# Hybrid encoder layer on Trainium2: the last input chunks and the branch and mixing weights loaded as 1 MB units with both halves of the split in one slot, and two expert chunks moved ahead of them in the load queue

## The chip, the cores and the metric

The kernel runs on one core of one Trainium2 chip. The metric is the device time of one execution in microseconds (us). The engines named below are TensorE (PE in the profile; PEld is its weight load), VectorE (DVE), ScalarE (ACT), GpSimd (POOL) and SyncE (SP), whose queue issues nearly all loads. All weights are read from HBM in every execution.

## The reference, cut to what is computed

```python
def token_mixer(h, ...):
    proj = h @ w_in + b_in
    q, k, v, xr, yr, gate_logits = jnp.split(proj, SPLITS, axis=-1)
    ...                                   # q/k norm, rotary positions
    attn = block_attention(q, k, v)
    xc = depthwise_conv(xr, conv_w, conv_b)
    lru = rglru(xc, ..., False) + rglru(xc, ..., True)
    rec = lru * jax.nn.gelu(yr, approximate=True)
    g_attn, g_rec = jnp.split(jax.nn.sigmoid(gate_logits), N_BRANCHES, axis=-1)
    merged = g_attn * (attn @ w_attn_o) + g_rec * (rec @ w_lru_o)
    return merged @ w_out
...
    x = x + token_mixer(rmsnorm(x, norm1_g[l]), ...)
    x = x + moe_ffn(rmsnorm(x, norm2_g[l]), ...)   # top 4 of 32 experts, SwiGLU
return rmsnorm(x, final_g)
```

x is 256 tokens by 1024 channels in float32. An expert has 1024x2048 weights going up and 1024x1024 going down, 12.6 MB; 32 experts are 402.7 MB of the 438 MB that are read.

## The kernel before, in words

**Buffers.** The ring is eight slots of 128x4096 float32 (2 MB each), numbered 0 to 7 and allocated in pairs (0,1), (2,3), (4,5), (6,7). LOWS is slot 6 and `wide` is slot 7. `late`, `pbuf`, `xr_flat` and `x_sb` hold other data first and expert weights later.

**First stage.** The mixer's weights come as 15 chunks of 128x4096 from `pre` (chunk 3 is half as wide). Chunks 0, 1 and 4 to 9 are the input projection, four blocks of output channels each: TensorE's `group(i)` for i = 0 to 31 computes block i%4 of its chunk, and `group_done` counts them. Chunks 2 and 3 are q, k and v. Chunks 10, 11 and 13 are the two branches' output matrices, 12 and 14 are `w_out`. Every chunk is split for precision into a high part, rounded to fp32r, and a low part, which is the rest: ScalarE makes the high part in two halves (`split_high`; VectorE does it for chunks 5 and 9), VectorE the low part (`split_low`), and `product` makes three matmuls out of each pair. The chunk lands in an even slot, its low part overwrites it there, and its high part goes into the odd slot beside it (for chunk 13: slot 6 and `late`).

**Around the change.** Chunks 4 to 9 are read by groups 8 to 31. Between the groups stand the attention's scores, transposes and values and the gates of the recurrence. Then TensorE runs `branches(g)` for g = 0 to 7, one block of 128 channels each; VectorE's loop over g multiplies both branch results with the gates, adds them and splits the sum (`merged_ok` counts these). `branches(g)` waits for `merged_ok` g-1, since it writes the PSUM bank of g-2. `mix(c)` multiplies block c of the merged sum into four PSUM banks, and `mix_end(n)` adds the last blocks to bank n. After that come the residual, the router, and the experts.

**Experts.** Expert weights are cut into chunks k of 2 MB, six an expert: four for gate and up, two for down. Chunk k goes to slot `SLOT_ORDER[k % 8]`; chunks 42, 43 and half of 41 have a place of their own in `late`, in `pbuf` and `xr_flat`, and in `x_sb`, and come early. From chunk 8 on `expert_load` waits until TensorE has read the chunk eight before it (`chunk_used`). Later, in the loop, two slots are loaded by one DMA of 4 MB.

**Order.** Each engine's order is written out by hand. SP issues its DMAs in that order and waits before each for what frees its place, so everything behind a waiting DMA waits too. VectorE and ScalarE likewise work strictly in order.

## Time and profile before

| what | value |
|---|---|
| median of 3 runs | 1138.17 us (1135.7 to 1138.58) |
| profiled execution, first to last instruction | 1134.2 us |
| TensorE busy | 1084.8 us (96%) |
| VectorE busy | 371.1 us (33%) |
| ScalarE busy | 237.2 us (21%) |
| read from HBM | 438.20 MB, 387 GB/s over the span |
| mean granted TensorE clock | 0.986 of full |

The metric is the time of a whole execution, the span runs from the first to the last instruction of one profiled execution; the median lies 4.0 us above that span. A share of busy time is an average over stages with different limits, so the stages have to be read one by one: the mixer's (up to about 211 us), the router's (211 to 226 us) and the experts' (from 226 us on). In the chain that ended last, each piece is what the next one waited for.

### The profile page before, as it was taken

Reading aid. Unit: us, or ns where it says so; the run is one execution under the profiler, and the core shown is the slowest. Engines: PE = TensorE matmul, PEld = TensorE weight load, DVE = VectorE, ACT = ScalarE, POOL = GpSimd, SP = SyncE. Lnnn points to the kernel's source line nnn. Section 1 sums busy time; section 2 is a strip of 40 time slices with the busy share of each in tenths; the row PEclk is TensorE's granted clock in tenths of the full one; section 3 lists DMA queues with packets and bytes.
Section 4 is the critical chain, followed back from the end, with each engine's and each line's share of the span. In section 5 each row is a group of like instructions: output and inputs, shape, how many; then the busy total and the mean of one; then the engine's idle time right before and its main releaser. Section 6 shows DMA issues by size and latency. Waiting matters only on the chain.

```text
span 1134.2 us, 12887 instructions
## 1 busy us (share of the span) xinstructions
PE 1084.8 (96%) x5407; PEld 503.4 (44%) x5407; DVE 371.1 (33%) x645; ACT 237.2 (21%) x369; POOL 2.6 (0%) x10
## 2 busy tenths in 40 slices
PE   7999999999999999999998989898989899899987
PEld 7999899633333333333333333333333333333332
DVE  6997887522212222122121211111211212121212
ACT  5399961211111111111111110011110101010102
POOL 0000000000000000000000000000000000000000
PEclk9999999899999999999999999999999999999999
DMA  9544277999999999999999999999999999999996
GB/s 353 185 178 149 84 287 300 419 425 399 431 425 428 426 434 432 433 426 435 431 429 436 430 430 436 429 430 436 430 432 433 429 436 430 427 427 429 426 428 247
DMA packets 25637, 439.77 MB, mean 388 GB/s; under 512 B 3425, under 2 KB 4065, under 8 KB 6273
## 3 DMA queue, kind: packets, MB, share of 16 engines
q1 hardware_dynamic: 24976, 438.27, 91.5%
q10 hardware_dynamic: 624, 0.99, 0.2%
q8 instruction: 27, 0.44, 0.2%
q14 instruction: 10, 0.07, 0.0%
HBM read 438.20 MB, written 1.05 MB: 387 GB/s over the span
## 4 chain that ended last, share of the span: by engine, by line
PE 67%; DMA 28%; DVE 2%; SPq 1%; ACT 1%; issue 0%; DVEq 0%
PE ps L1491 26%; DMA slots<-in_w_down_dram 22%; PE ps L1500 13%; PE ps L1172 13%; DMA slots<-in_w_gu_dram 5%; PE ps L1455 5%; PE ps L1436 3%; PE ps L1549 2%; DVE slots_r L725 1%; SPq L403 1%; PE ps L1229 1%; PE ps L1450 1%; PE ps L1414 1%; PE ps L1234 0%; PE ps L1526 0%; PE ps L1274 0%
## 5 line engine op out<-in xcount | busy, mean ns | idle before, releaser
L1500 PE MATMUL ps<-slots,lru 128*64 128x512 f32 x1024 | 239.8, 610 | 17.2 <-DMA slots<-in_w_down_dram 17.2
L1491 PE MATMUL ps<-slots,lru 128*64 128x512 f32 x1024 | 227.7, 594 | 11.7 <-DMA slots<-in_w_gu_dram 11.2
L1491 PE MATMUL ps<-slots,qT 128*64 128x512 f32 x984 | 223.8, 596 | 4.6 <-DMA slots<-in_w_gu_dram 4.6
L1491 PEld LDWEIGHTS ps<-slots,lru 128*64 128x64 f32 x1024 | 74.1, 137 | 160.8 <-issue 139.7
L1491 PEld LDWEIGHTS ps<-slots,qT 128*64 128x64 f32 x984 | 68.9, 137 | 152.2 <-issue 144.8
L1500 PEld LDWEIGHTS ps<-slots,lru 128*64 128x64 f32 x1024 | 68.5, 139 | 142.5 <-issue 123.5
L1100 DVE COPY lru<-ps 128x512 f32<-128x512 f32 x32 | 22.1, 692 | 322.9 <-PE ps L1491 322.9
L1172 PE MATMUL ps<-slots_r 128*128 128x256 f32 (+1 forms) x812 | 107.7, 291 | 0.2 <-DVE slots_r L725 0.2
L1172 PEld LDWEIGHTS ps<-slots_r 128*128 128x128 f32 x812 | 102.2, 191 | 5.4 <-issue 2.5
L653 ACT ACTIVATE lru<-ps 128x512 f32<-128x512 f32 x32 | 19.1, 598 | 395.3 <-PE ps L1491 395.3
L1082 DVE TENSOR_SCALAR lru<-sq,rank_col,small 128x64 f32<-128x64 f32 x64 | 17.2, 312 | 241.8 <-PE ps L1436 241.8
L1455 PE MATMUL ps<-lru 128*128 128x512 f32 x136 | 65.5, 605 | 0.9 <-DVE lru L1135 0.9
L1108 DVE TENSOR_TENSOR lru<-ps,cst 128x1024 f32<-128x1024 f32 x32 | 39.2, 1225 | 74.3 <-PE ps L1549 74.3
L1436 PE MATMUL ps<-hn,lru 128*64 128x512 f32 x256 | 62.7, 608 | 0.9 <-DVE lru L1020 0.9
L725 DVE TENSOR_TENSOR slots_r<-slots,slots_r 128x4096 fp32r<-128x4096 f32 (+1 forms) x16 | 62.0, 3888 | 3.6 <-ACT slots_r L440 3.4
L645 ACT ACTIVATE lru<-ps 64x512 f32<-64x512 f32 x63 | 37.3, 592 | 123.0 <-PE ps L1500 122.3
L655 ACT ACTIVATE lru<-lru 128x512 f32<-128x512 f32 x32 | 20.2, 631 | 149.6 <-DVE lru L1112 149.6
L440 ACT ACTIVATE slots_r<-slots 128x2048 fp32r<-128x2048 f32 (+1 forms) x24 | 43.4, 1840 | 36.5 <-DMA slots<-in_pre_dram 36.5
L638 ACT ACTIVATE qT<-ps 128x512 f32<-128x512 f32 x32 | 19.1, 598 | 137.5 <-PE ps L1436 137.5
L1549 PEld LDWEIGHTS ps<-sq,lru 128*128 128x128 f32 x256 | 34.8, 197 | 29.3 <-DVE lru L1100 18.5
L1549 PE MATMUL ps<-sq,lru 128*128 128x128 f32 x256 | 41.9, 314 | 0.0
L1455 PEld LDWEIGHTS ps<-lru 128*128 128x128 f32 x136 | 23.2, 190 | 31.5 <-issue 29.7
(200 smaller groups left out, 649.3 us busy)
## 6 DMA issues: line engine op xcount, KB each, us to landing
slots<-in_w_gu_dram SPq DMA_DIRECT2D x40, 4096.0 KB, 29.2
slots<-in_w_gu_dram SPq DMA_DIRECT2D x44, 2048.0 KB, 18.9
slots<-in_w_down_dram SPq DMA_DIRECT2D x20, 4096.0 KB, 28.4
slots<-in_w_down_dram SPq DMA_DIRECT2D x22, 2048.0 KB, 20.8
slots<-in_pre_dram SPq DMA_DIRECT2D x13, 2048.0 KB, 8.2
slots<-in_w_down_dram SPq DMA_DIRECT2D x8, 512.0 KB, 31.0
slots<-in_pre_dram SPq DMA_DIRECT2D x3, 1024.0 KB, 6.9
slots<-in_w_gu_dram SPq DMA_DIRECT2D x3, 1024.0 KB, 17.4
```

The costliest lines, as they stand in the source:

```text
L440: nc.scalar.activation(high(c)[:, i * w:(i + 1) * w], whole(c)[:, i * w:(i + 1) * w], ACT.Copy).then_inc(split_hi, 1)
L645: nc.scalar.activation(pair_out[i // 2 % 2][rs, side * BANK:(side + 1) * BANK], ps[64 * side:64 * side + 64, bank, :], ACT.Copy).then_inc( ...
L655: nc.scalar.activation(as3(sig), gv[:, :, 0, :], ACT.Sigmoid, scale=ALPHA).then_inc(sig_ok, 1)
L725: return nc.vector.tensor_tensor(dst, whole, hi.bitcast(f32), ALU.subtract)
L1100: nc.vector.tensor_copy(gu_sb[:, 0:BANK], ps[:, 4, :]).then_inc(gu_v, 1)
L1108: nc.vector.tensor_tensor(gub.rearrange("p (j n) -> p j n", j=16), ps[:, 4:6, :].rearrange("p b (j n) -> p (b j) n", n=CAP), bias.unsqueez ...
L1172: ins = nc.tensor.matmul(dst, st[a], mv[b], start=start and q == 0 and k == 0, stop=stop and q == 2 and k == len(sides) - 1)
L1436: ins = nc.tensor.matmul(ps[64 * h:64 * h + 64, 7, :], sel_next[:, t, :], x2[:, t, h * BANK:(h + 1) * BANK], start=(t == 0), stop=(t == T ...
L1455: return nc.tensor.matmul(ps[:, n, :], sgT[pair][:, n // 2, :], pair_out[pair][:, (n % 2) * BANK:(n % 2 + 1) * BANK], start=False, stop=last)
L1491: ins = nc.tensor.matmul(ps[64 * side:64 * side + 64, 4 + b, :], xgT[i % 2][:, k, :], rows[r][:, o:o + BANK], start=(k == 0), stop=(k == K ...
L1500: ins = nc.tensor.matmul(ps[64 * side:64 * side + 64, bank, :], actT[(i - 1) % 2][:, k, :], w[:, r, side * BANK:(side + 1) * BANK], start= ...
L1549: ins = nc.tensor.transpose(ps[:, 4 + j // 4, j % 4 * P:(j % 4 + 1) * P], gu_sb[:, j::KD], ident)
```

## The change

1. Chunks 0 to 7 stay as they are. Chunks 8 to 14 become 14 units of 1 MB, two a chunk, each in one slot: it lands in the slot's first half, where its low part overwrites it, and its high part goes into the second half. Units 0 to 3 are chunks 8 and 9 (groups 24 to 31), units 4 to 9 the branch weights, units 10 to 13 `w_out`.
2. A half of chunk 8 or 9 is 256 columns out of each 512, so that units 0 to 3 are read from HBM in rows of 1 KB.
3. Units 0 to 7 use slots 4, 5, 0, 1, 4, 5, 0, 1. That leaves the pair (2,3) free when chunk 7 has been read, and expert chunks 0 and 1 are issued there, after `group_done` 24, ahead of units 4 to 13.
4. SP's order, what each load waits for, and `SLOT_ORDER` change with it. The load of `late` and that of `pbuf` now stand ahead of unit 7.
5. VectorE's low parts come one unit at a time after the merge of each g but 3, where before a whole chunk came after g = 1, 3 and 7.
6. TensorE runs `branches(0)` to `branches(7)` in a row and then `mix(0)` to `mix(5)`, where `mix(0)` stood after `branches(3)`; `mix_end` has two blocks a bank instead of four. The number of matmuls is the same.

```diff
-        SLOT_ORDER = [2, 3, LOWS, SLOTS - 1, 0, 1, 4, 5]
-        EARLIER = [5, 0, 4, 0, 5, 0, 1, 1]
-        FREED = {2: [(branch_ps, 3)], 0: [(mixed_ps, 1)], LOWS: [(branch_ps, KD)], 4: [(mixed_ps, 2)]}
+        CHUNKS, UNIT = 8, CH // 2
+        PLACE = [2 * (c % PAIRS) for c in range(CHUNKS)]
+        UNITS = [(8, 0), (8, 1), (9, 0), (9, 1), (10, 0), (10, 1), (11, 0), (11, 1), (13, 0), (13, 1),
+                 (12, 0), (12, 1), (14, 0), (14, 1)]
+        UNIT_SLOT = [4, 5, 0, 1, 4, 5, 0, 1, LOWS, 4, 5, 0, 1, LOWS]
+        UNIT_FREED = [(group_done, 16), (group_done, 16), (group_done, 20), (group_done, 20), (group_done, 26),
+                      (group_done, 28), (group_done, 30), (group_done, 32), (gate_ps, 32), (branch_ps, 2),
+                      (branch_ps, 3), (branch_ps, 4), (branch_ps, 6), (branch_ps, 7)]
+        BR_UNIT, MIX_UNIT = 4, 10
+
+        SLOT_ORDER = [2, 3, 4, 5, 0, 1, LOWS, SLOTS - 1]
+        EARLIER = [PLACE.count(s) + UNIT_SLOT.count(s) for s in range(SLOTS - 1)] + [1]
+        FREED = {2: (group_done, 24), 4: (branch_ps, KD), 5: (mixed_ps, 1), 0: (mixed_ps, 2), 1: (mixed_ps, 3),
+                 LOWS: (mixed_ps, 4)}
...
-            for c in range(1, PRE):
-                if c == 13:
-                    sp.wait_ge(group_done, 32)
-                    sp.wait_ge(gate_ps, 32)
-                elif c == 14:
-                    sp.wait_ge(pv_ps, NQ // 2)
-                    half_load(extra_rows(1, 0), EXTRA[1], 0, extra_full[1])
-                    half_load(wide[:, 0:2048], 3, 0, slot_full[SLOTS - 1])
-                    for k in range(2):
-                        expert_load(k)
-                    sp.wait_ge(branch_ps, 6)
-                elif c >= PAIRS:
+            def unit_load(u):
+                sp.wait_ge(*UNIT_FREED[u])
+                dst = kn(unit_whole(u)) if u < BR_UNIT else unit_whole(u)
+                sp.dma_start(dst, unit_src(u)).then_inc(slot_full[UNIT_SLOT[u]], 16)
+
+            for c in range(1, CHUNKS):
+                if c >= PAIRS:
                     sp.wait_ge(*CONSUMED[c - PAIRS])
...
-            expert_load(2)
-            half_load(wide[:, 2048:], 3, 1, slot_full[SLOTS - 1])
+            for u in range(4):
+                unit_load(u)
+            for k in range(2):
+                expert_load(k)
+            for u in range(4, 7):
+                unit_load(u)
+            sp.wait_ge(rec_ok, 2)
+            sp.wait_ge(pv_ps, NQ // 2)
             n, j = step_of(EXTRA[0])
             sp.dma_start(late[:, :], expert_src(n, j)).then_inc(extra_full[0], 16)
-            for k in (4, 5):
-                expert_load(k)
+            half_load(extra_rows(1, 0), EXTRA[1], 0, extra_full[1])
+            unit_load(7)
+            unit_load(8)
+            half_load(wide[:, 0:2048], 7, 0, slot_full[SLOTS - 1])
+            for u in range(9, 14):
+                unit_load(u)
+            expert_load(2)
+            half_load(wide[:, 2048:], 7, 1, slot_full[SLOTS - 1])
             sp.wait_ge(merged_ok, KD)
             half_load(extra_rows(1, 1), EXTRA[1], 1, extra_full[1])
-            for k in RING_CHUNKS[6:SLOTS]:
+            for k in range(3, SLOTS - 1):
                 expert_load(k)
...
             recurrent_high(0)
-            split_high(10, [0])
+            unit_split_high(4)
             group_pair(26)
             pair_probs(3)
-            split_high(10, [1])
+            unit_split_high(5)
             group_pair(28)
             recurrent_high(1)
-            split_high(11, [0])
             attention_high()
+            unit_split_high(6)
             group_pair(30)
-            split_high(11, [1])
             load_sqrt_table(2)
-            for c in range(12, PRE):
-                split_high(c)
+            for u in range(7, len(UNITS)):
+                unit_split_high(u)
...
-            split_low(10)
+            unit_split_low(4)
+            unit_split_low(5)
             recurrent_low(1)
             attention_low()
-            split_low(11)
+            unit_split_low(6)
...
-                if g == 1:
-                    split_low(12)
-                if g == 3:
-                    split_low(13)
-                if g == KD - 1:
-                    split_low_by_halves(14)
+                if g != 3:
+                    unit_split_low(7 + g if g < 3 else 6 + g)
...
-            BLOCKS = CH // P
-            w_br = [chunk(c, BLOCKS) for c in BR_CHUNK]
+            BLOCKS = UNIT // P
+
+            w_br = [unit(u, BLOCKS) for u in range(BR_UNIT, MIX_UNIT)]
...
-                for i, c in enumerate(BR_CHUNK[:2]):
-                    if g > 0 and first <= BLOCKS * i < first + 12:
-                        chunk_in(c)
...
+                u = BR_UNIT + (first + KD - 1) // BLOCKS
...
+                product(half(4 + g % 2, 1), recurrent, ahead=((unit_high_ok(u),), (unit_low_ok(u),), ()))
+                u = BR_UNIT + (first + 11) // BLOCKS
+                product(half(4 + g % 2, 0), attention, ahead=((unit_high_ok(u),), (unit_low_ok(u),), ())
+                        ).then_inc(branch_ps, 1)
+
+            ENDS = 6
...
-                if c == 3:
+                if c % 2 == 1:
                     ins.then_inc(mixed_ps, 1)
...
             def mix_end(n):
-                for c in range(4, KD):
+                if n == 0:
+                    pe.wait_ge(*unit_low_ok(MIX_UNIT + 3))
+                for c in range(ENDS, KD):
...
-            for g in range(4):
+            for g in range(KD):
                 branches(g)
-            mix(0)
-            for g in range(4, KD):
-                branches(g)
-            for c in range(1, 4):
+            for c in range(ENDS):
                 mix(c)
```

The load queue before, from chunk 10 of the mixer's weights (first row) on. slots0 to slots3 are the four pairs, `in_pre` the mixer's weights, `in_w_gu` an expert's:

```order
L339 DMA slots0<-in_pre_dram 128x4096 [waits group_done]
L339 DMA slots1<-in_pre_dram 128x4096 [waits group_done]
L339 DMA slots2<-in_pre_dram 128x4096 [waits group_done]
L339 DMA slots0<-in_pre_dram 128x4096 [waits group_done]
L339 DMA slots3<-in_pre_dram 128x4096 [waits lru_gate_ps,group_done]
L324 DMA pbuf<-in_w_gu_dram 128x2048 [waits pv_ps]
L324 DMA slots3<-in_w_gu_dram 128x2048
L320 DMA slots1<-in_w_gu_dram 128x4096 [waits branch_ps]
L320 DMA slots1<-in_w_gu_dram 128x4096
L339 DMA slots2<-in_pre_dram 128x4096 [waits branch_ps]
L320 DMA slots3<-in_w_gu_dram 128x4096 [waits branch_ps]
```

And now, from units 0 and 1 (first row):

```order
L361 DMA slots2<-in_pre_dram 128x8x256 [waits group_done] x2
L361 DMA slots0<-in_pre_dram 128x8x256 [waits group_done] x2
L352 DMA slots1<-in_w_gu_dram 128x4096 [waits group_done]
L352 DMA slots1<-in_w_gu_dram 128x4096
L361 DMA slots2<-in_pre_dram 128x2048 [waits group_done] x2
L361 DMA slots0<-in_pre_dram 128x2048 [waits group_done]
L396 DMA late<-in_w_gu_dram 128x4096 [waits pv_ps,recurrent_ok]
L356 DMA pbuf<-in_w_gu_dram 128x2048
L361 DMA slots0<-in_pre_dram 128x2048 [waits group_done]
L361 DMA slots3<-in_pre_dram 128x2048 [waits lru_gate_ps]
L356 DMA slots3<-in_w_gu_dram 128x2048
L361 DMA slots2<-in_pre_dram 128x2048 [waits branch_ps] x2
```

Two expert chunks now stand right behind unit 3, and 3 MB for `late` and `pbuf` stand between unit 6 and unit 7 (the row that waits for group_done again).

VectorE before, from the low part of chunk 11 (the second chunk of branch weights) to that of chunk 12. The five 128x256 rows are one merge:

```order
L725 TENSOR_TENSOR slots2_r<-slots2,slots2_r 128x4096 [waits chunk_high]
L961 SCALAR_TENSOR_TENSOR lru<-hn,ps 128x256 [waits branch_ps]
L963 SCALAR_TENSOR_TENSOR lru<-xr_flat,ps 128x256
L965 TENSOR_TENSOR lru<-lru 128x256 [waits v_step]
L722 CAST lru_r<-lru 128x256 [waits v_step]
L725 TENSOR_TENSOR lru_r<-lru,lru_r 128x256 [waits v_step]
L961 SCALAR_TENSOR_TENSOR lru<-hn,ps 128x256 [waits branch_ps]
L963 SCALAR_TENSOR_TENSOR lru<-xr_flat,ps 128x256
L965 TENSOR_TENSOR lru<-lru 128x256 [waits v_step]
L722 CAST lru_r<-lru 128x256 [waits v_step]
L725 TENSOR_TENSOR lru_r<-lru,lru_r 128x256 [waits v_step]
L725 TENSOR_TENSOR slots0_r<-slots0,slots0_r 128x4096 [waits chunk_high]
```

And now, from the low part of unit 6 to the second merge:

```order
L764 TENSOR_TENSOR slots0_r<-slots0,slots0_r 128x2048 [waits chunk_high]
L1004 SCALAR_TENSOR_TENSOR lru<-hn,ps 128x256 [waits branch_ps]
L1006 SCALAR_TENSOR_TENSOR lru<-xr_flat,ps 128x256
L1008 TENSOR_TENSOR lru<-lru 128x256 [waits v_step]
L761 CAST lru_r<-lru 128x256 [waits v_step]
L764 TENSOR_TENSOR lru_r<-lru,lru_r 128x256 [waits v_step]
L764 TENSOR_TENSOR slots0_r<-slots0,slots0_r 128x2048 [waits chunk_high]
L1004 SCALAR_TENSOR_TENSOR lru<-hn,ps 128x256 [waits branch_ps]
L1006 SCALAR_TENSOR_TENSOR lru<-xr_flat,ps 128x256
L1008 TENSOR_TENSOR lru<-lru 128x256 [waits v_step]
L761 CAST lru_r<-lru 128x256 [waits v_step]
L764 TENSOR_TENSOR lru_r<-lru,lru_r 128x256 [waits v_step]
```

A low part, that of unit 7, now stands between the first merge and the second; before, both merges stood ahead of the next low part.

## Rows read from the trace of the kernel before

**Rows 1.** Page, section 2: what all DMA moved, in 40 slices of 28.4 us
```profile
GB/s 353 185 178 149 84 287 300 419 425 399 431 425 428 426 434 432 433 426 435 431 429 436 430 430 436 429 430 436 430 432 433 429 436 430 427 427 429 426 428 247
```

**Rows 2.** Stages: length, each engine's busy us (count), TensorE clock, DMA share, GB/s
```profile
165.00:211.00 46.00, 46.00 (x303) 42.27 (x302) 30.21 (x45) 10.69 (x9) 0.00 (x0) 1.00 0.86 345
211.00:226.00 15.00, 13.69 (x67) 7.29 (x65) 8.77 (x34) 4.61 (x10) 0.00 (x0) 0.77 1.00 421
226.00:276.00 50.00, 49.79 (x218) 17.41 (x220) 13.79 (x37) 5.31 (x8) 0.00 (x0) 1.00 1.00 410
276.00:531.00 255.00, 255.00 (x1165) 89.51 (x1160) 53.97 (x108) 28.49 (x48) 0.00 (x0) 1.00 1.01 429
531.00:1080.00 549.00, 518.67 (x2311) 185.76 (x2310) 112.39 (x220) 57.79 (x96) 0.00 (x0) 0.98 1.00 431
```

**Rows 3.** Chain that ended last, 500 to 640 us: start, us, what
```profile
527.51 3.61 PE ps L1491 x16
531.27 26.39 DMA slots<-in_w_down_dram
```

**Rows 4.** Timeline of the load queue: issue start, us, what, count
```profile
250.46 5.48 SPq L320 DMA_DIRECT2D slots<-in_w_gu_dram  x2
261.28 5.83 SPq L320 DMA_DIRECT2D slots<-in_w_down_dram  x2
272.18 3.76 SPq L320 DMA_DIRECT2D slots<-in_w_gu_dram  x2
```

**Rows 5.** Loads issued at 250.46, 266.78, 272.18, 275.62: count, KB, us to landing
```profile
slots<-in_w_gu_dram SPq DMA_DIRECT2D x1, 2048.0 KB, 8.7
slots<-in_w_down_dram SPq DMA_DIRECT2D x1, 2048.0 KB, 8.5
slots<-in_w_gu_dram SPq DMA_DIRECT2D x1, 2048.0 KB, 8.0
slots<-in_w_gu_dram SPq DMA_DIRECT2D x1, 2048.0 KB, 9.5
```

**Rows 6.** Same view: issued at 124.09, 63.06, 154.57 and 155.04
```profile
slots<-in_pre_dram SPq DMA_DIRECT2D x1, 2048.0 KB, 7.8
slots<-in_w_lru_dram SPq DMA_DIRECT2D x1, 1024.0 KB, 4.8
pbuf<-in_w_gu_dram SPq DMA_DIRECT2D x1, 1024.0 KB, 15.4
slots<-in_w_gu_dram SPq DMA_DIRECT2D x1, 1024.0 KB, 17.4
```

**Rows 7.** Timeline of VectorE: start, us, line, what, shapes, count, [idle before]
```profile
156.41 4.42 DVE L725 TENSOR_TENSOR slots_r<-slots,slots_r 128x4096 fp32r<-128x4096 f32 x1 [1.58 <-ACT slots_r L440]
160.76 0.41 DVE L961 SCALAR_TENSOR_TENSOR lru<-hn,ps 128x256 f32<-128x256 f32 x1
162.32 0.43 DVE L725 TENSOR_TENSOR lru_r<-lru,lru_r 128x256 fp32r<-128x256 f32 x1
193.73 4.49 DVE L725 TENSOR_TENSOR slots_r<-slots,slots_r 128x2048 fp32r<-128x2048 f32 x2
```

**Rows 8.** Timeline of ScalarE, same columns
```profile
140.15 0.84 ACT L460 ACTIVATE xr_flat<-ps,cst 128x256 f32<-128x256 f32 x2
154.46 1.92 ACT L440 ACTIVATE slots_r<-slots 128x2048 fp32r<-128x2048 f32 x1
```

**Rows 9.** Timeline of TensorE, same columns
```profile
146.67 1.08 PE L1298 MATMUL ps<-pbuf,late 128*64 128x256 f32 x8
147.68 6.01 PE L1172 MATMUL ps<-slots_r 128*128 128x256 f32 x48
153.53 2.08 PE L1172 MATMUL ps<-lru_r,slots_r 128*128 128x256 f32 x16
157.85 2.08 PE L1172 MATMUL ps<-lru_r,slots_r 128*128 128x256 f32 x16
162.89 2.14 PE L1172 MATMUL ps<-lru_r,slots_r 128*128 128x256 f32 x16 [0.56 <-DVE lru_r L725]
```

More of the change, by code:

```diff
@@ L578, in _ @@
             lru_gates(1, [0])
-            split_high(8, [0])
+            unit_split_high(0)
             pair_exps(0)
@@ L1177, in chunk, with unit @@
                 return [b.rearrange("p (k n) -> p k n", k=k) for b in (high(c), low(c))]
+            def unit(u, k):
+                return [b.rearrange("p (k n) -> p k n", k=k) for b in (unit_high(u), unit_low(u))]
             def transposes(rows, tp0):
```

103 lines of the change are left out of this document (59 added, 44 removed).

## The prediction

> **What bounds the kernel now.** I read the GB/s line of the page first. From the eighth slice on (199 us) the DMA moves 399 to 436 GB/s to the end [rows 1]: all weights have to come in, and the end is the moment at which the last of them can have come. The stages say more [rows 2]. From 276 us on the DMA is busy all the time at 429 to 431 GB/s. TensorE is too until 531 us (255.00 of 255.00 us); after that it waits 30 us in 549. The chain that ended last is TensorE until 531.1 us and a load from 531.27 us on [rows 3]. So the experts' stage is bound by the DMA once its queue is full, and the question is when that begins. It doesn't begin at 199 us: between 226 and 276 us the DMA makes 410 GB/s, 19 below the 429 that follow, 0.95 MB or 2.2 us of idle, while TensorE is busy 49.79 of 50 us [rows 2].
>
> The load queue shows why [rows 4, 5]. A load of 2 MB with nothing ahead of it lands after 7.8 us [rows 6]. Those issued at 250.46, 266.78 and 272.18 us land after 8.7, 8.5 and 8.0 us, so next to nothing stands ahead of them, and they are issued when TensorE frees their slots: each waits for a `chunk_used`. The one issued at 275.62 lands after 9.5 us, at 285.1, which is 4.9 us behind the 280.2 of the one before. From there the queue grows. **The pinch is at 266 to 272 us**: there the end is set by the moment at which TensorE gives back a slot, and from there by 4.9 us for each 2 MB. TensorE is at that point at the end of an unbroken row of work: 46.00 of 46 us in the mixer, 13.69 of 15 in the router, 49.79 of 50 in the first experts [rows 2].
>
> **The change part by part.**
>
> *The head start.* Expert chunks 0 and 1 are issued at `group_done` 24, 124.1 us (where chunk 10 is issued now), instead of at `branch_ps` 3, 162.89 + 4.3 = 167.2 us [rows 9]. That is 4 MB, or 2 x 4.9 = 9.8 us of DMA work moved into time in which the DMA idles. 13 MB are then left of what is loaded before chunk 8 (21 MB in all, of which chunks 0 and 1, `late`, `pbuf` and half a chunk in `wide` have landed). The first 2 MB are issued when the branches end, near 189.5 us, and land at 197.3; the other 11 MB at 2.45 us each end near 224.3 us. Chunk 8, though, waits for TensorE to have read chunk 0, some 4 us after 226 us (16 matmuls of a chunk take 3.6 us [rows 3]). The DMA has nothing to do between 224.3 and 230, and at 250 to 272 us it waits for slots as before, only longer. I price the head start at nothing: the load at 272.18 us can't be issued earlier than its slot is read, and it now lands within 8.0 - 7.8 = 0.2 us of what an empty queue gives. Bounds: 0 to -0.2 us. What counts is only how far TensorE's timeline moves.
>
> *Units 0 to 3.* Read in rows of 1 KB instead of 16 KB. No row shows 1 KB rows in bulk. They are issued with the 2 MB loads that they replace, units 2 and 3 at `group_done` 20, and unit 3 is used by group 30, ten groups or at least 29 us later (two groups take 6.0 us [rows 9]). Even a landing three times as long as the usual 7.8 us is in time. Nothing, bounds 0 and 0; the ten groups are the cover.
>
> *Units 4 to 6.* Unit 4 waits for `group_done` 26, near 131 us (124.1, some values of 1.1 and two groups of 6.0), and lies behind the two expert chunks: 124.1 + 7.8 = 131.9, 136.8 for the second, 139.3 for the unit. ScalarE waits for it and casts for 1.92 us [rows 8] to 141.2; its copies of groups 26 and 27 then come 1.1 us later than the 140.15 of now. TensorE needs them for group 30, at 147.7 [rows 9]. Nothing. Unit 5 lands at 140.1 + 4.8 = 144.9 [rows 6], unit 6 at 146.7 + 4.8 = 151.5, both cast before groups 30 and 31 end at 153.6.
>
> *The low parts after the groups.* Now VectorE starts chunk 11's low part at 156.41, after a wait of 1.58 for ScalarE, and ends at 160.8; the merge that follows ends at 162.75, and TensorE starts `branches(2)` at 162.89 [rows 7, 9]. Its step is 157.85 - 153.53 = 4.32 us, so it was ready at 162.17: 0.72 us lost. With units, the low part of unit 6 is done at 157.1 (half the work, ScalarE's cast ends at 153.4) and the first merge at 160.0. **-0.72 us.**
>
> *The low part of unit 7, ahead of the second merge.* This is new. Unit 7 may be issued at `group_done` 32, 153.7 us, when `late` (2 MB) and `pbuf` (1 MB), issued at 147.8 when the last values end [rows 9], stand ahead of it. `late` lands 4.9 us behind unit 6, at 156.4; `pbuf` at 158.9; unit 7 at 161.4 (a queued 1 MB costs 155.04 + 17.4 - 154.57 - 15.4 = 2.5 us [rows 6]). ScalarE's cast ends at 163.3, VectorE's low part of 2.25 us (half of 4.49 [rows 7]) at 165.6. Only then comes the second merge, 162.75 - 160.76 = 1.99 us, to 167.6. `branches(3)` waits for it; TensorE is ready at 162.17 + 4.32 = 166.49 and starts at 167.75 (0.14 us after the merge, as now). **+1.26 us**, which nothing hides. If the unit lands up to 1.26 us earlier the stall is gone; 1 us later, it is 2.3.
>
> *The later units.* Per g VectorE has 1.99 + 2.25 = 4.24 us of work less 0.1 of overlap against TensorE's 4.32: it keeps up but gains nothing back. Unit 8 lands at 163.9, unit 9 (issued at 162.3, half a chunk ahead) at 168.9, 10 to 13 when `branch_ps` 3, 4, 6 and 7 are up, 4.8 us later each: all cast before their turn. `branches(4)` needs the third merge at 171.9 and is ready at 172.1. Bounds 0 to +1 us; I take 0, as the sum leaves 0.2 to 0.3 us a step.
>
> *The order of mix.* The same matmuls in another order. `mix_end` has half the work a bank, so VectorE's residuals of 1.1 us follow each other at 1.3 us instead of 2.6; the last still starts when the last bank ends. Nothing; up to +0.3 us if the transposes wait for the second residual.
>
> *A rule on sizes.* The halves of 1 MB queue at 2.5 us each, 421 GB/s [rows 6]. The Trainium skill (DMA: Bandwidth & Descriptors, section Bandwidth) gives 341 GB/s for 1 MB and speaks for larger transfers, which is against this change. By it `pbuf` and unit 7 would each take 3.1 us, the stall would be 2.5 us instead of 1.26, and the time 1.2 us longer; the trace doesn't bear it out for queued loads.
>
> **The sum.** -0.72 + 1.26 = +0.54 us at the pinch, and the same at the end, since all behind it is DMA at a fixed pace: 1134.2 + 0.5 = 1134.7 us for the profiled span. The median of the runs lies 4.0 us above that span, and the runs themselves spread over 2.9 us: 1138.17 + 0.5 = 1138.7 us.
>
> **The rivals.**
>
> *A, my forecast (0.58).* A stall of about 1.3 us moves from one branch to the next and the head start is lost at the pinch: 1138.7 us.
>
> *B, no new stall (0.20).* Unit 7 comes earlier, or VectorE is quicker. TensorE gains 0.72 and the pinch up to 0.2 more: 1137.3 us. For it: landings of single loads differ by half a microsecond.
>
> *C, the head start lasts (0.08).* If the DMA were the bound from 199 us on, as the GB/s line alone suggests, 9.8 us would come off: 1128.4 us. Against it stand the 410 GB/s before 276 us and the landings of 8.0 to 8.7 us. For it: TensorE would have to reach its first experts earlier too, which only a clock that stays up in the router's stage could give: it is at 0.77 there over 15 us [rows 2], so at 1.2 GHz for some 6.9 us, worth up to 3.4 us.
>
> *D, slower (0.14).* TensorE falls to 1.2 GHz once more. Its clock fell in this trace during the router's stage, behind thin work with gaps of under 1 us. A stall of 1.26 us at 166.5 us, with others added if VectorE's margin of 0.2 us a step doesn't hold, may do the same within the branches, where every matmul is on the path. A fall as long as that one costs half of 6.9 us: 0.5 + 3.4 = +3.9, 1142.1 us. It decides from a stall that is long enough to make the clock fall; the present 0.72 us did not.
>
> **How the numbers follow.** A measurement of this kernel can tell 0.3% (3.4 us) from no change: below 1134.8 is faster, above 1141.6 slower. A and B lie within (0.78), C is faster (0.08), D slower (0.14). The range takes in A and B with the spread of the runs (1135.7 to 1138.6 around the median) and the unit's landing 1 us late or more: 1135.5 to 1141.5 us.
>
> **What would show it.** In the profile after: a wait of TensorE for VectorE's merge near 166.5 us, of about 1.3 us, and none at 162.2; expert chunks 0 and 1 issued near 124 us; a DMA that idles near 225 to 230 us and moves fewer than 410 GB/s between 226 and 276 us; loads there that land after 7.8 to 8 us; and the same 429 to 431 GB/s behind it. I am wrong if the load that is issued at 272.2 us now is issued more than 2 us earlier or later, or if the gap between 276 us and the end changes.

## The result and the profile after

| | before | after |
|---|---|---|
| median | 1138.17 us (1135.7 to 1138.58) | 1141.87 us (1140.9 to 1142.57) |
| ratio | 1 | 1.0039, 95% interval 1.0028 to 1.0049 |
| profiled execution, first to last instruction | 1134.2 us | 1140.4 us |
| TensorE's first matmul on chunk 0 | 13.65 us | 13.78 us |
| TensorE begins the experts | 226.21 us | 229.84 us |
| load at the pinch lands | 280.19 us | 285.68 us |

The change makes the kernel 0.39% slower, 4.4 us by the ratio, where 0.5 us were predicted; it came out in the direction of rival D, and a little beyond the range. Both medians are of five runs; the three of before in the table ahead are among them. The profiled execution of after took 1142.15 us as a whole, 1.75 above its span, so of the 4.0 us between span and median of before some 2.2 us are a profiled execution that lay at the fast end of its runs. The 6.2 us between the two spans are therefore not the effect; the ratio is. Two executions far off all others, one of before beside the less_mix kernels below (2821.02 us) and one of merges_first_long_rows (1226.41 us), are left out of the ratios.

First TensorE in the branches, from the timeline of after (start, us, what, count, idle before it and what ended it):

```profile
162.29 2.08 PE L1211 MATMUL ps<-lru_r,slots_r 128*128 128x256 f32 x16
164.21 1.12 PE L1211 MATMUL ps<-slots_r 128*128 128x256 f32 x8
165.17 1.12 PE L1211 MATMUL ps<-lru_r,slots_r 128*128 128x256 f32 x8
166.13 0.64 PE L1211 MATMUL ps<-qT_r,slots_r 128*128 128x256 f32 x4
169.28 3.02 PE L1211 MATMUL ps<-lru_r,slots_r 128*128 128x256 f32 x16 [2.51 <-DVE lru_r L764]
172.10 1.81 PE L1211 MATMUL ps<-slots_r 128*128 128x256 f32 x8
...
175.18 2.08 PE L1211 MATMUL ps<-lru_r,slots_r 128*128 128x256 f32 x16
```

The wait of [rows 9] at 162.89 is gone: `branches(2)` starts at 162.29, 0.6 us sooner. `branches(3)` could start its recurrent part 0.48 us behind 166.13, at 166.61, and starts at 169.28: 2.67 us lost, where +1.26 stood in the sum. And its matmuls behind the wait take 3.02 us for 16 where 2.08 was usual. The windows show why; the columns are busy us (count) of TensorE, its weight loads, VectorE, ScalarE and GpSimd, then granted clock, DMA share and GB/s:

```profile
170.30:173.60 3.30, 3.30 (x18) 3.30 (x17) 3.20 (x7) 1.91 (x1) 0.00 (x0) 0.50 0.30 122
221.50:228.20 6.70, 5.72 (x14) 1.35 (x15) 3.88 (x17) 0.99 (x3) 0.00 (x0) 0.50 0.99 413
...
230.00:233.40 3.40, 3.40 (x18) 1.11 (x18) 1.73 (x12) 0.00 (x0) 0.00 (x0) 1.00 0.00 0
234.50:280.00 45.50, 45.50 (x200) 15.87 (x198) 11.72 (x23) 5.66 (x9) 0.00 (x0) 1.00 0.99 388
280.00:531.00 251.00, 251.00 (x1148) 88.35 (x1144) 54.05 (x108) 28.12 (x47) 0.00 (x0) 1.00 1.01 430
```

TensorE's clock fell to half (1.2 of 2.4 GHz) 1.0 us behind the end of the 2.5 us wait. It was at half from 170.25 to 173.66, 3.41 us. `branches(4)` starts 175.18 - 169.28 = 5.90 us behind `branches(3)` where 4.32 is usual, so the fall costs 1.6 us. The fall in the router's stage is there as before, 6.83 us long. From 230.0 to 233.4 us no DMA moves anything, and from 280 on it moves the 430 GB/s of before.

What ended VectorE's wait, and ScalarE's ahead of it:

```profile
159.74 0.43 DVE L764 TENSOR_TENSOR lru_r<-lru,lru_r 128x256 fp32r<-128x256 f32 x1
165.02 2.29 DVE L764 TENSOR_TENSOR slots_r<-slots,slots_r 128x2048 fp32r<-128x2048 f32 x1 [4.85 <-ACT slots_r L481]
167.23 0.41 DVE L1004 SCALAR_TENSOR_TENSOR lru<-hn,ps 128x256 f32<-128x256 f32 x1
...
168.80 0.43 DVE L764 TENSOR_TENSOR lru_r<-lru,lru_r 128x256 fp32r<-128x256 f32 x1
```

```profile
163.08 1.91 ACT L481 ACTIVATE slots_r<-slots 128x2048 fp32r<-128x2048 f32 x1 [6.88 <-DMA slots<-in_pre_dram]
165.57 1.91 ACT L481 ACTIVATE slots_r<-slots 128x2048 fp32r<-128x2048 f32 x1 [0.58 <-DMA slots<-in_pre_dram]
```

VectorE has nothing to do from 160.17 to 165.02 but to wait for unit 7's high part, and the second merge (167.23 to 169.23) stands behind its low part. ScalarE waited for the load. The loads of `late`, `pbuf` and unit 7 were issued at 147.97, 148.34 and 153.84 us:

```profile
late<-in_w_gu_dram SPq DMA_DIRECT2D x1, 2048.0 KB, 8.9
...
pbuf<-in_w_gu_dram SPq DMA_DIRECT2D x1, 1024.0 KB, 12.2
...
slots<-in_pre_dram SPq DMA_DIRECT2D x1, 1024.0 KB, 9.2
```

They landed at 156.89, 160.57 and 163.06 us. Unit 7 is 2.49 behind `pbuf`, as the sum has it, but `pbuf` is 3.68 behind `late` instead of 2.5. What the DMA did in these 3.7 us:

```profile
DMA packets 205, 1.56 MB, mean 421 GB/s; under 512 B 16, under 2 KB 16, under 8 KB 16
## 3 DMA queue, kind: packets, MB, share of 16 engines
q1 hardware_dynamic: 204, 1.54, 99.2%
q8 instruction: 1, 0.02, 1.7%
```

It was not slower: 421 GB/s, 1.56 MB for a load of 1 MB. A load counts as landed when the last of the 16 engines is done with its share, and the trace has a time for each: for `pbuf` 15 were done by 159.38 us, within 0.7 us of one another, and the last at 160.57. Unit 7 shows the same, 161.88 and 163.06, and so do the two loads behind it; one engine stays 1.2 us behind while the others go on. One 16 KB packet of instructions (q8) stood in this stretch; the packet records put it at 157.71 us with 1.02 us, where a packet of the weights takes 0.61. The same 3.3 to 4.0 us, with one engine 0.8 to 1.7 us behind and an instruction packet at 156.4 to 157.8, are in the eight kernels below that keep this order of loads. That this packet is the cause is read from the times; no run moves it. It doesn't always show: in before one of 1.02 us at 174.43 us left the interval of two loads at 4.89, since one engine was already 1.0 us behind (at 161.53 and 162.56 the last two were done with the load issued at 153.72). The 2.5 us of [rows 6] are intervals of loads that all carry that same delay.

Last, the loads issued at 254.09, 264.91, 275.81 and 279.25 us, which answer to [rows 5]:

```profile
slots<-in_w_gu_dram SPq DMA_DIRECT2D x1, 2048.0 KB, 10.0
...
slots<-in_w_down_dram SPq DMA_DIRECT2D x1, 2048.0 KB, 10.1
...
slots<-in_w_gu_dram SPq DMA_DIRECT2D x1, 2048.0 KB, 9.9
...
slots<-in_w_gu_dram SPq DMA_DIRECT2D x1, 2048.0 KB, 11.3
```

With the two between them (issued at 259.24 and 270.41) they take 9.9 to 10.3 us up to the pinch, where 8.0 to 8.9 were usual. So the pinch moves by more (5.5 us) than TensorE does (3.6).

### The profile page after: what moved, and what is told of

It reads as the page before. It is cut to its first block, busy times and chain, and to the rows that moved or that the text cites. A ratio compares the mean times of both kernels' runs of the same rounds, so it can differ in the third digit from the quotient of the medians.

```text
span 1140.4 us, 12909 instructions
## 1 busy us (share of the span) xinstructions
PE 1081.7 (95%) x5407; PEld 502.0 (44%) x5407; DVE 372.3 (33%) x652; ACT 237.8 (21%) x369; POOL 2.3 (0%) x10
## 4 chain that ended last, share of the span: by engine, by line
PE 66%; DMA 29%; DVE 2%; SPq 1%; ACT 1%; issue 0%; DVEq 0%
PE ps L1536 26%; DMA slots<-in_w_gu_dram 15%; PE ps L1211 13%; PE ps L1545 13%; DMA slots<-in_w_down_dram 12%; PE ps L1500 5%; PE ps L1481 3%; PE ps L1594 2%; SPq L442 1%; DVE slots_r L764 1%; PE ps L1276 1%; PE ps L1495 1%; DMA slots<-in_pre_dram 1%; PE ps L1460 1%; PE ps L1281 1%; PE ps L1571 0%
## 5 line engine op out<-in xcount | busy, mean ns | idle before, releaser
L1536 PEld LDWEIGHTS ps<-slots,lru 128*64 128x64 f32 x1024 | 71.7, 137 | 165.0 <-issue 134.5
L1545 PEld LDWEIGHTS ps<-slots,lru 128*64 128x64 f32 x1024 | 67.8, 137 | 139.9 <-issue 112.4
L1211 PE MATMUL ps<-slots_r 128*128 128x256 f32 (+1 forms) x832 | 111.1, 293 | 0.2 <-DVE slots_r L764 0.2
L1211 PEld LDWEIGHTS ps<-slots_r 128*128 128x128 f32 x832 | 105.6, 193 | 5.4 <-issue 2.9
L764 DVE TENSOR_TENSOR slots_r<-slots,slots_r 128x2048 fp32r<-128x2048 f32 (+1 forms) x23 | 67.2, 2938 | 7.0 <-ACT slots_r L481 6.6
L1594 PE MATMUL ps<-sq,lru 128*128 128x128 f32 x256 | 38.9, 298 | 0.0
L1481 PEld LDWEIGHTS ps<-hn,lru 128*64 128x64 f32 x256 | 19.4, 139 | 35.4 <-issue 34.4
```

The costliest lines, as they stand in the source:

```text
L764: return nc.vector.tensor_tensor(dst, whole, hi.bitcast(f32), ALU.subtract)
L1211: ins = nc.tensor.matmul(dst, st[a], mv[b], start=start and q == 0 and k == 0, stop=stop and q == 2 and k == len(sides) - 1)
L1481: ins = nc.tensor.matmul(ps[64 * h:64 * h + 64, 7, :], sel_next[:, t, :], x2[:, t, h * BANK:(h + 1) * BANK], start=(t == 0), stop=(t == T ...
L1536: ins = nc.tensor.matmul(ps[64 * side:64 * side + 64, 4 + b, :], xgT[i % 2][:, k, :], rows[r][:, o:o + BANK], start=(k == 0), stop=(k == K ...
L1545: ins = nc.tensor.matmul(ps[64 * side:64 * side + 64, bank, :], actT[(i - 1) % 2][:, k, :], w[:, r, side * BANK:(side + 1) * BANK], start= ...
L1594: ins = nc.tensor.transpose(ps[:, 4 + j // 4, j % 4 * P:(j % 4 + 1) * P], gu_sb[:, j::KD], ident)
```

## The experiments

All kernels do the reference's work whole but the two named "less_mix". Differences are ratios to before, each measured beside runs of before on the same chip. A start of the experts is counted from TensorE's first matmul on chunk 0, since that lay anywhere between 12.65 and 14.39 us in the profiled executions.

### Which wait costs it: VectorE's order

Theory T: the low part of unit 7 ahead of the second merge makes the wait, the wait makes the clock fall, and the rest is as before. Rival R: the added transfers and short rows cost it anyway. Four kernels are after with one edit. `merges_first` keeps both first merges ahead of the low part:

```diff
-                if g != 3:
-                    unit_split_low(7 + g if g < 3 else 6 + g)
+                if g > 0:
+                    unit_split_low(6 + g)
```

> The kernel after, with VectorE's second merge ahead of the low part of unit 7 (low parts 7 to 13 after the merges of g = 1 to 7); no load is touched. T: the second merge ends near 164.4 us, TensorE has no wait in the branches, the clock stays up, experts from 225.5 us on, 1137.5 us. R: no load changes, so nothing changes: 1141.9.

Measured: 1136.68 us (1135.79 to 1137.76), ratio 0.9996 (0.9986 to 1.0006). The wait is gone; the timeline of TensorE:

```profile
165.31 1.12 PE L1211 MATMUL ps<-lru_r,slots_r 128*128 128x256 f32 x8
166.27 0.64 PE L1211 MATMUL ps<-qT_r,slots_r 128*128 128x256 f32 x4
166.75 2.08 PE L1211 MATMUL ps<-lru_r,slots_r 128*128 128x256 f32 x16
168.67 1.12 PE L1211 MATMUL ps<-slots_r 128*128 128x256 f32 x8
```

T holds: one line of VectorE's order is worth 0.43%, 4.9 us, and the transfers and 1 KB rows that R blames are still there. Yet nothing is won over before, although the experts begin 1.4 us sooner; more of that below. Of the 1.4 us, 0.8 lie ahead of the router, near the 0.72 predicted for the low parts; the other 0.6 are the router's stage, where the clock fell for 3.41 us in this execution and for 6.83 in that of before.

`stall_filled` leaves the wait and gives TensorE 22 transposes of the identity into a free bank in it:

```diff
             for g in range(KD):
+                if g == 3:
+                    filler(2, 22)
                 branches(g)
```

> The kernel after, with 22 transposes of the identity into an unused bank between branches(2) and branches(3), some 2.4 us of TensorE work that fills the wait for the second merge. T with the clock as a part of it: the wait is filled and the clock doesn't fall at 170 us; experts from 228.3 us on instead of 229.8, the time 1.5 us shorter, 1140.4. If the fall of the clock cost nothing: 1141.9, or more by what the filler overruns. R: 1141.9.

Measured: 1139.92 us (1138.71 to 1141.55), ratio 1.0028 (1.0018 to 1.0038). Timeline and windows:

```profile
166.59 2.56 PE L1421 MATMUL ps<-sq 128*128 128x128 f32 x22
169.32 2.18 PE L1211 MATMUL ps<-lru_r,slots_r 128*128 128x256 f32 x16 [0.17 <-DVE lru_r L764]
...
173.74 2.08 PE L1211 MATMUL ps<-lru_r,slots_r 128*128 128x256 f32 x16
```

```profile
170.00:174.00 4.00, 4.00 (x36) 4.00 (x35) 3.90 (x7) 2.89 (x2) 0.00 (x0) 1.00 0.30 121
224.60:227.90 3.30, 2.94 (x10) 1.24 (x10) 0.90 (x4) 0.27 (x1) 0.00 (x0) 0.50 0.70 283
```

The branches wait as long as in after, behind work that nobody needs, and the clock stays up: `branches(4)` starts 4.42 us behind `branches(3)`, not 5.90. The wait, then, makes the clock fall. By the ratios 1.3 us come off, with two intervals that just overlap (1.0028 to 1.0049 and 1.0018 to 1.0038). The experts begin 2.0 us sooner: 1.4 of it is there when mix begins, and 0.6 comes in the router's stage, where the fall is 3.41 us long instead of 6.83 in this execution, which the edit doesn't touch. So of the 3.5 us by which the experts of after are late, 1.4 to 1.6 are the clock's fall in the branches; the rest is the wait, less the 0.72 won.

`unit7_first` loads units 7 and 8 ahead of `late` and `pbuf`:

```diff
+            unit_load(7)
+            unit_load(8)
             sp.wait_ge(rec_ok, 2)
...
             half_load(extra_rows(1, 0), EXTRA[1], 0, extra_full[1])
-            unit_load(7)
-            unit_load(8)
```

> The kernel after, with the loads of units 7 and 8 issued ahead of those of late and pbuf. Theory T (the end follows the moment at which TensorE reaches the experts): unit 7 lands near 158.7 us, the 2.5 us wait of TensorE for the second merge is gone, the clock doesn't fall near 170 us, the experts start near 225.5 us instead of 229.8, and the time is 0.6 us under the kernel before: 1137.5. Rival R (the loss lies in the loads: rows of 1 KB, halves of 1 MB, a queue that runs dry): the loads are the same in number and size and two of the large ones come later, so the time stays at 1141 to 1143.

Measured: 1145.28 us (1143.8 to 1146.86), ratio 1.0068 (1.0046 to 1.009), 8 us away from what I expected. Timelines of TensorE and of VectorE:

```profile
180.93 3.79 PE L1211 MATMUL ps<-lru_r,slots_r 128*128 128x256 f32 x16 [5.79 <-DVE lru_r L764]
```

```profile
176.67 2.29 DVE L764 TENSOR_TENSOR slots_r<-slots,slots_r 128x2048 fp32r<-128x2048 f32 x1 [6.53 <-ACT slots_r L481]
```

The first wait is gone. But the 3 MB now stand ahead of unit 9, which lands at 174.70 instead of 170.50 and whose low part stands ahead of the fourth merge: the same wait two units later, twice as long, with the clock at half for 6.83 us from 179.93, 1.0 us before the wait ends. I had looked only at the unit that was late.

`chunks_late` takes the head start back, with the two expert chunks behind unit 9:

```diff
-            for k in range(2):
-                expert_load(k)
             for u in range(4, 7):
...
-            for u in range(9, 14):
+            unit_load(9)
+            for k in range(2):
+                expert_load(k)
+            for u in range(10, 14):
```

> The kernel after, with expert chunks 0 and 1 issued behind unit 9, near 162 us, instead of near 124 us. T: the head start of 4 MB is worth nothing as long as TensorE reaches the experts when it does; unit 4 lands 3 us sooner, unit 7 where it did; the stall stays, 1141.9 us within 1. If the head start were worth its bytes (9.8 us), the time would be 1151. R: a queue that runs dry less in front of the experts would give some of its loss back, 1139 to 1141.

Measured: 1143.23 us (1142.43 to 1143.87), ratio 1.0055 (1.0036 to 1.0073). The wait stays, 2.76 us, so the head start doesn't cause it; a second of 0.85 us comes at 189.02, behind unit 10, which stands behind the two chunks now. The same edit on merges_first:

> merges_first with expert chunks 0 and 1 issued behind unit 9 instead of ahead of unit 4. T alone: experts from 225.1 us on, or 0.9 us later if unit 10 is late for its low part; 1136.7 to 1137.6 us as merges_first. Rival Q (a queue that runs dry costs by itself: merges_first starts its experts 1.1 us sooner than the kernel before and is no faster): here the DMA isn't idle at 226 to 229 us any more, the loads at 250 to 276 us land after 8 to 9 us instead of 9.2 to 10, and 1.4 us come off, 1135.3.

Measured: 1144.01 us (1143.47 to 1144.98), ratio 1.007 (1.005 to 1.0089), far off. Timelines of TensorE, VectorE and ScalarE:

```profile
188.36 3.78 PE L1212 MATMUL ps<-lru_r,slots_r 128*128 128x256 f32 x16 [5.16 <-DVE lru_r L765]
```

```profile
184.11 2.29 DVE L765 TENSOR_TENSOR slots_r<-slots,slots_r 128x2048 fp32r<-128x2048 f32 x1 [7.29 <-ACT slots_r L482]
```

```profile
182.16 1.91 ACT L482 ACTIVATE slots_r<-slots 128x2048 fp32r<-128x2048 f32 x1 [10.36 <-DMA slots<-in_pre_dram]
```

Unit 10 lands at 182.14, TensorE comes to the merge behind it sooner, waits 5.16 us, and the clock falls within the wait, at 185.57, for 6.83. As a test of the head start both kernels are spoiled; as a test of the mechanism they are three more cases of it.

`before_low_early` makes the same wait in the kernel before, by order alone: the low part of chunk 12 after g = 0 instead of g = 1.

```diff
-                if g == 1:
+                if g == 0:
                     split_low(12)
```

> The kernel before, with the low part of chunk 12 ahead of VectorE's second merge instead of behind it; no load is touched. T: the chunk lands at 162.6 us, its cast ends at 166.3, its low part at 170.8, the second merge at 172.8; branches(3) starts 5.5 us late (172.9 instead of 167.3), and the clock falls for 3.4 or 6.8 us, 1.7 or 3.4 us more: the time is 6 to 9 us longer, 1142.5 to 1145.5 where the kernel before has 1136.3. R (loads alone decide): 1136.3.

Measured: 1145.28 us (1143.83 to 1146.06), ratio 1.0075 (1.0055 to 1.0095). TensorE waits from 166.88 to 172.52, and the clock is at half for 6.83 us from 168.75, 3.1 us of it behind the wait:

```profile
162.33 2.15 PE L1172 MATMUL ps<-lru_r,slots_r 128*128 128x256 f32 x16 [0.56 <-DVE lru_r L725]
...
172.52 3.52 PE L1172 MATMUL ps<-lru_r,slots_r 128*128 128x256 f32 x16 [5.64 <-DVE lru_r L725]
```

### Where the head start goes

Theory S: TensorE's freeing of slots sets the pace at the pinch, so that 4 MB more in place are worth nothing as long as TensorE begins no sooner. The test is to make it begin sooner, in both kernels, by leaving one of the three products out of every `mix` (32 matmuls of 128x512, 6.9 us; `product` skips the terms that are not named).

```diff
-                               start=(c == 0), stop=(c == KD - 1))
+                               start=(c == 0), stop=(c == KD - 1), terms=(0, 2))
```

> The kernel before, with the low part of the merged sum left out of the mix: 32 of the 96 matmuls of 128x512 less, 32 x 0.216 = 6.9 us of TensorE work less (the output lacks that term). Experts from 219.3 us on instead of 226.2. Theory T (the end follows the moment at which TensorE reaches the experts, as long as the loads before are done by then): here the DMA is still busy with the loads ahead of the experts until 234.5 us, so the 6.9 us can't all be passed on; what it loses at 250 to 276 us comes back, 2 to 3 us: 1133.5 to 1134.5 us where the kernel before has 1136.3. If the end followed TensorE alone: 1129.4.

> merges_first with the same 32 matmuls left out of the mix (the output lacks that term). Experts from 218.2 us on instead of 225.1. T with the head start: the 4 MB that come early are worth something only now, since the DMA would have finished the loads ahead of the experts by some 226 us: the 6.9 us are passed on nearly whole, 1130 to 1131 us where merges_first has 1136.7. If the head start were worth nothing in any case, this kernel and before_less_mix would gain the same.

Measured: before_less_mix 1132.9 us (1131.86 to 1133.89), ratio 0.9964 (0.995 to 0.9978); merges_first_less_mix 1128.48 us (1128.17 to 1129.54), ratio 0.9933 (0.9914 to 0.9953). Without the head start 4.1 us come back of 4.8 by which the experts begin sooner; with it 7.6 of 7.5 (against merges_first 7.2 of 6.1). The two kernels differ by 3.5 us in time and by 2.7 in the start of the experts, so the times alone don't show a worth of the head start.

The landings do. Counted from TensorE's first matmul on chunk 0, the load at the pinch lands at 266.54 us in before and 264.88 in before_less_mix, 1.7 sooner; it lands at 266.37 in merges_first and 259.79 in merges_first_less_mix, 6.6 sooner. In before_less_mix the loads follow one another without a gap from 234.58 us on: the DMA is the bound there. So the head start has a worth, and it is only seen when TensorE comes early enough to use it. From that landing to the end of the span it is 853.3 to 854.9 us in all fourteen profiled executions, so the landing at the pinch decides the span. (The profiled pair of before and before_less_mix is accordingly 2.1 us apart; the ratio says 4.1 with an interval of 3 us. This isn't settled better.)

The pace of the DMA between 234.5 and 280 us, in one window of before, before_less_mix, merges_first, merges_first_less_mix, and merges_first_reload (below), same columns as above:

```profile
234.50:280.00 45.50, 45.50 (x200) 15.84 (x198) 10.73 (x19) 5.52 (x8) 0.00 (x0) 1.00 1.00 407
```

```profile
234.50:280.00 45.50, 45.50 (x200) 15.82 (x198) 11.72 (x23) 6.11 (x9) 0.00 (x0) 1.00 1.01 428
```

```profile
234.50:280.00 45.50, 45.50 (x200) 15.83 (x198) 11.03 (x21) 5.83 (x9) 0.00 (x0) 1.00 0.99 391
```

```profile
234.50:280.00 45.50, 45.50 (x200) 15.71 (x200) 10.82 (x22) 5.23 (x8) 0.00 (x0) 1.00 0.99 402
```

```profile
234.50:280.00 45.50, 45.50 (x200) 15.84 (x198) 11.66 (x23) 6.13 (x9) 0.00 (x0) 1.00 0.99 391
```

The engines are busy all the time in all of them, and yet move 388 (in after) to 428 GB/s: at the start of a load single packets of 16 KB take over 0.8 us instead of 0.61, 64 of them in before, up to 1.3 us, and 84 in merges_first, up to 2.6. In before_less_mix, where each load is issued over 6 us before the one ahead of it lands (these take 11 to 13 us), there are 3, and every load lands 4.88 to 4.91 us behind the last. In the others, with loads issued 2 to 5 us ahead, it is anything from 4.9 to 7.3. A deep queue is no warrant: in merges_first a load issued at 286.55 us, 8.4 ahead, landed 6.23 behind the last, with one engine 1.3 us behind the others and an instruction packet at 298.61. Between before and merges_first the windows differ by 16 of 407 GB/s over 45.5 us, 1.8 us, and it eats the 1.4 us that TensorE gains: the load at the pinch lands only 0.17 us sooner.

Theory Q: this comes from the queue's having stood empty from 226 to 230 us. `merges_first_reload` keeps it full there by reading 2 MB twice:

```diff
             half_load(x_flat, HALF, 1, half_full)
+            sp.wait_ge(extra_full[1], 32)
+            half_load(extra_rows(1, 1), EXTRA[1], 1, extra_full[1])
+            half_load(extra_rows(1, 0), EXTRA[1], 0, extra_full[1])
```

> The kernel merges_first (1136.7) with two more loads of 1 MB behind the half chunk for x_sb: the two halves of chunk 43 are read once more into the places where they already lie, and TensorE waits for the second copies before it uses that chunk, at the end of the loop's first eight experts. Nothing is left out. In merges_first the queue stood empty from 226.2 to 229.8 us, and the first expert loads behind that gap landed 5.3 to 6.7 us after one another instead of 4.9; with the two loads the queue has work until 231. Theory Q (the empty queue itself costs, as slow first packets): the loads issued at 249 to 271 us land 8 to 9 us after their issue again, and the time is 1135.3, less than without the added 2 MB. Theory S (up to 280 us the pace is set by the slots that TensorE frees, whatever the queue did ahead): 1136.7 within 0.4, the added 5 us of transfers cost nothing. If the transfers themselves were the bound, with no slack for 2 MB: 1138 to 1141.

Measured: 1136.63 us (1134.6 to 1137.58), ratio 0.9993 (0.9984 to 1.0002). S: 2 MB more, 5 us of transfers, and no time lost. Q falls: the queue had work until 229.94 us, and the loads issued at 259.57 and 265.07 still take 10.1 and 10.2 us, at 391 GB/s as in merges_first, though the two ahead of them take 7.9 and 8.9 where merges_first has 9.4 and 9.6. What makes the packets slow when a load follows closely on the one ahead stays open.

### The router's clock, and the short rows

`merges_first_router_filled` and `before_router_filled` have 26 transposes of the identity in TensorE's waits in the router's stage.

```diff
             logits(0, range(KD))
+            filler(7, 7)
             second_transposes(1)
...
+            filler(7, 3)
             pe.wait_ge(sel_ok, 1)
             gather_tile(0)
+            filler(3, 6)
             ranks(1)
+            filler(3, 6)
             pe.wait_ge(sel_ok, T)
...
+            filler(3, 2)
             gathered_transposes(0)
...
+            filler(3, 2)
             step(0, 0, True)
```

> merges_first with 26 transposes of the identity into a free bank in the router's stage, in TensorE's waits there, so that its clock may stay up; nothing is left out. In merges_first the granted clock was at half for one stretch of 3.41 us, 221.78 to 225.19, and the experts began at 225.12. Theory S (the time follows the moment at which TensorE begins the experts, by 0.94 us a us): with the clock up the experts begin 0.9 to 1.7 us sooner, 223.4 to 224.2, and the time is 1135.1 to 1135.8. Theory Q (the loads behind the empty queue set the pace, not TensorE): 1136.7 within 0.4. If the transposes delay the gate instead and the clock falls all the same: 1137 to 1138.5.

> The kernel before with the same 26 transposes in the router's stage; nothing is left out. Before had its clock at half for 6.83 us, 217.73 to 224.56. If the clock stays up, the experts begin up to 3.4 us sooner than 226.21; here the loads cannot come sooner (the queue is full until 234.55, then nine loads of 4.89: 278.6 instead of the 280.19 at the pinch). Theory S with that bound: 1.5 to 2.9 us less than before (the kernel with less mixing began 4.75 us sooner and took 4.0 less). If only half of the stretch is avoided, 1 to 1.5 less. If the clock's price was nothing to the end: within 0.5 of before.

Measured: 1138.03 us (1135.1 to 1139.54), ratio 1.0006 (0.9997 to 1.0015); and 1136.61 us (1135.05 to 1140.47), ratio 0.9996 (0.9987 to 1.0005). The windows from 215 us to the experts, of merges_first without and with the transposes:

```profile
215.00:226.00 11.00, 8.79 (x42) 4.13 (x42) 6.88 (x33) 2.44 (x6) 0.00 (x0) 0.84 0.86 359
```

```profile
215.00:226.00 11.00, 10.51 (x65) 5.80 (x65) 7.08 (x36) 1.89 (x6) 0.00 (x0) 1.00 0.73 304
```

The clock stays at full, 1.00 instead of 0.84, and still the experts begin 211.76 us behind the first matmul on chunk 0 instead of 211.19. The stage is a chain of TensorE and VectorE by turns, and the transposes stand in it: they cost what the clock gives. In before the fall shrinks from 6.83 to 3.41 us, and the experts begin 1.5 us later, not sooner; the stage itself, from the end of mix to the experts, takes 15.98 us instead of 14.48 (14.43 instead of 13.87 in merges_first). No gain in either, so my step from "the clock is up" to "TensorE is early" was wrong here.

`merges_first_long_rows` lays units 0 to 3 out so that they are read in rows of 8 KB:

```diff
...
-                dst = kn(unit_whole(u)) if u < BR_UNIT else unit_whole(u)
-                sp.dma_start(dst, unit_src(u)).then_inc(slot_full[UNIT_SLOT[u]], 16)
+                sp.dma_start(unit_whole(u), unit_src(u)).then_inc(slot_full[UNIT_SLOT[u]], 16)
...
+    rest[4:] = [r.reshape(P, KD, 2, TOK).transpose(0, 2, 1, 3) for r in rest[4:]]
```

> merges_first with the halves of the last two input chunks laid out in device memory as they are loaded, so that units 0 to 3 are read in rows of 8 KB and not of 1 KB; nothing is left out. Theory of the prediction (the short rows are hidden): units 2 and 3 land 1 to 2 us sooner behind one another than the 4.25 us between them now, nothing waits for them, and the time stays 1136.7 within 0.5. Rival: if the 4096 short packets cost the rest of the stage transfers, 0.5 to 1.5 less.

Measured: 1136.59 us, ratio 0.9997 (0.9987 to 1.0007). Units 2 and 3, issued at 103.9 and 104.3 us, land at 109.03 and 112.56 instead of 109.78 and 114.14. The short rows cost up to 1.6 us of a transfer, and nothing of the time.

### All kernels in one table

| kernel | experts begin, against before | time, against before |
|---|---|---|
| merges_first_less_mix | -7.5 us | -7.6 us |
| before_less_mix | -4.8 | -4.1 |
| merges_first | -1.4 | -0.5 |
| merges_first_long_rows | -1.3 | -0.3 |
| merges_first_reload | -0.8 | -0.8 |
| merges_first_router_filled | -0.8 | +0.7 |
| before_router_filled | +1.5 | -0.5 |
| stall_filled | +1.5 | +3.2 |
| after | +3.5 | +4.4 |
| chunks_late | +5.3 | +6.3 |
| merges_first_chunks_late | +6.4 | +8.0 |
| before_low_early | +7.6 | +8.5 |
| unit7_first | +8.2 | +7.7 |

Both columns carry 1 us of uncertainty or more: the first is one execution each, the second has intervals of 2 to 5 us. For the two router_filled kernels the first column is no guide to the median, since the profiled execution of merges_first_router_filled was its fastest (1135.1 us) and that of before_router_filled its slowest (1140.47). Within that, the time goes with the moment at which the experts begin, in kernels with and without the head start. No version that does all the work beats before by more than a measurement can tell.

## Why the prediction was wrong

**Right.** That TensorE's timeline, not the number of bytes, decides at the pinch once the head start is there, which reload and the table show; for before itself it is less sharp, since nine loads of 4.89 us behind 234.55 would land at 278.6 at best, and 280.19 was measured. That the head start of 4 MB is worth nothing by itself (merges_first). That units 0 to 6 are hidden: unit 4 lands at 138.75 (139.3 predicted), unit 5 at 145.50 (144.9), unit 6 at 151.87 (151.5). The -0.72 of the low parts behind the groups: the wait at 162.2 is gone. The place of the new wait. That the DMA has an idle stretch, though it ran from 230.3 to 233.5, 3.2 us, instead of from 224.3 to 230. The 429 to 431 GB/s behind the pinch. The order of mix: nothing waits there. That the rule on sizes doesn't hold for queued loads: by the 341 GB/s of the Trainium skill (DMA: Bandwidth & Descriptors, section Bandwidth) a queued 1 MB would take 3.1 us. Unit 7, unit 8 and half a chunk landed 2.49, 2.49 and 2.48 behind one another. The rule gave a wait of 2.5 us, near the 2.67 measured, but for a reason that these intervals exclude: luck.

**Wrong, the size of the new wait** ("+1.26", measured +2.67). The step that failed is the chain of landings. It had `late` at 156.4 and `pbuf` 2.5 us behind it; `late` came at 156.89 and `pbuf` 3.68 behind, so the second merge ended at 169.23 instead of 167.6. I took the interval of two loads from [rows 6] as a constant; it is one only as long as no engine of the 16 falls behind. I had written that 1 us later makes 2.3 us, and took it as an edge of the range instead of pricing it.

**Wrong, the clock** (0 in the sum, 0.14 as rival D; measured 1.6 us by the step of the branches, 1.4 by stall_filled). 2.51 us of waiting made it fall, 0.56 us in [rows 9] hadn't, and neither had the 0.85 us at 189.02 of chunks_late. What a wait of the predicted 1.26 us would have done no run shows. The two errors hang together: by rival D's own condition, "a stall that is long enough", the doubled wait may be what made D come true. The fall was half as long as the one that I priced (3.41 instead of 6.83 us); in before_low_early and unit7_first, with waits of 5.64 and 5.79 us, it is 6.83. That D's 1142.1 us lies so near the median is luck: its wait was half the real one and its fall twice.

**Wrong, the DMA at the pinch** ("8.0 - 7.8 = 0.2 us", measured about +1.9 in the profiled pair, near 1 by the ratios). I took 7.8 us as what an empty queue gives, read the 8.7, 8.5 and 8.0 of [rows 5] as loads with next to nothing ahead, and the 19 GB/s missing before 276 us as idle. [rows 2] shows a DMA share of 1.00 there: it was slow packets, not idle engines. The loads of [rows 5] were issued 3.7, 2.7 and 3.1 us before the one ahead of each landed. A load of 2 MB alone in the queue does land after 7.2 to 7.9 us from 120 us on, but those issued 2 to 5 us ahead of the last one's landing mostly take 8 to 10. So the load that was issued at 272.18 us is now issued at 275.81, past the 2 us that I had named as a sign of being wrong.

The sum with the measured terms: -0.72 + 2.67 + 1.6 = 3.55 us, the 3.5 by which the experts begin later. The time grew by 4.4 (by the ratio), the landing at the pinch by 5.4 (in the profiled pair, both counted from the first matmul on chunk 0); the 0.9 to 1.9 left over are the DMA's pace, and why its packets are slow there stays open.

## What to carry to other kernels

Work that is put between two steps of a tight chain (here a 2.3 us low part between two merges) turns the landing time of its input into a deadline: compute the slack of every later item behind the same loads, not only of the one that is late, since moving loads merely moves the wait to the next. If a sum comes to a wait of some 2.5 us on a TensorE that is otherwise unbroken, price the clock's fall as part of the wait; here waits up to 1.03 us did nothing, and between 1.03 and 2.51 us nothing was measured. A window in which the DMA's share is full and its GB/s are low has slow packets, not idle time. 4 MB of head start didn't mend that here; where the loads were issued over 6 us ahead (before_less_mix) it was gone.
